# Gate projection spread over the inversion levels, and 64-row blocks for the GLA and RWKV states

## The reference

```python
u = rmsnorm(h, norm_mix);  proj = u @ w_in
y_rw  = rwkv7_mix(token_shift(proj[:, :1792]))     # 8 heads x 64
y_gla = gla_mix(proj[:, 1792:])                    # 4 heads, key 64, value 128
h = h + concat(y_rw, y_gla) @ w_out
h = h + moe(rmsnorm(h))                            # top 4 of 32 experts, 12.6 MB of weights each
h = h + sigmoid(rmsnorm(h) @ w_ple_gate) * (p @ w_ple);  out = rmsnorm(h)
# gla_mix, per chunk of 64 tokens:
o = (q * exp(b)) @ state + (tril(decayed q k^T)) @ v
state = exp(b_last) * state + (k * exp(b_last - b))^T @ v
o = o * rsqrt(mean(o*o)) * norm_g * silu(g)        # g: the 512 gate columns of proj
# rwkv7_mix, per token:
state = state * w + (state @ -kk) (kk*a)^T + v k^T;  o = state @ r
```

## Time and profile before

| | us |
|---|---|
| runs (3): median, lowest, highest | 1190.81, 1190.02, 1194.16 |
| the profiled execution | 1189.66 |
| its span from first to last instruction | 1187.9 |
| TensorE busy | 1121.3 |
| VectorE, ScalarE, GpSimd busy | 322.1, 217.9, 45.7 |
| HBM read in all | 430.57 MB |

### The profile page before, as it was taken

How to read it: one execution, slowest core, us unless ns; L and a number is a source line. 1 busy time by engine, 2 the same in 40 slices (tenths; PEclk the granted TensorE clock), 3 DMA queues, 4 the chain that set the end, 5 groups by cost and what they waited for, 6 DMA issues and landing times.

```text
span 1187.9 us, 15866 instructions
## 1 busy us (share of the span) xinstructions
PE 1121.3 (94%) x6255; PEld 504.7 (42%) x6255; DVE 322.1 (27%) x727; ACT 217.9 (18%) x394; POOL 45.7 (4%) x97
## 2 busy tenths in 40 slices
PE   8999899999999999998999889899999999999997
PEld 6876675433333433333333333333333333333344
DVE  2362366322222212122121221222222222222233
ACT  3233220221111111111111111111121111111124
POOL 8004200000000000000000000000000000000000
PEclk9999998999999999999999999999999999999999
DMA  9500328989999999999999999999999999999960
GB/s 326 196 1 1 135 100 336 359 353 429 429 428 429 428 429 428 429 428 430 426 430 427 429 428 429 428 429 427 430 428 429 428 428 429 427 429 428 428 282 37
DMA packets 41979, 432.11 MB, mean 364 GB/s; under 512 B 5300, under 2 KB 8696, under 8 KB 16824
## 3 DMA queue, kind: packets, MB, share of 16 engines
q1 hardware_dynamic: 41696, 431.34, 86.7%
q10 hardware_dynamic: 248, 0.29, 0.1%
HBM read 430.57 MB, written 1.05 MB: 363 GB/s over the span
## 4 chain that ended last, share of the span: by engine, by line
PE 57%; DMA 39%; DVE 1%; ACT 1%; issue 1%; POOL 1%; ACTq 0%; SPq 0%; DVEq 0%; POOLq 0%
PE ps L1209 53%; DMA ring<-in_w_dram 38%; PE ps L1752 1%; PE ps L1690 1%; DMA ay<-in_norm_ple_dram 0%; PE ps L1737 0%; PE ps L1624 0%; ACT ring L669 0%; ACTq L543 0%; PE ps L1454 0%; PE ps L1236 0%; PE ps L1608 0%; SPq L314 0%; PE ps L1333 0%; POOL ring L508 0%
## 5 line engine op out<-in xcount | busy, mean ns | idle before, releaser
L1209 PE MATMUL ps<-ring,ay 128*64 128x512 f32 x1024 | 245.4, 623 | 35.9 <-DMA ring<-in_w_dram 34.4
L1209 PE MATMUL ps<-ring,gqk 128*64 128x512 f32 x1024 | 224.3, 596 | 6.2 <-DMA ring<-in_w_dram 5.2
L1121 DVE COPY t<-ps 128x512 f32<-128x512 f32 x32 | 22.1, 691 | 505.7 <-PE ps L1209 505.7
L1209 PEld LDWEIGHTS ps<-ring,ay 128*64 128x64 f32 x1024 | 73.1, 142 | 183.7 <-issue 135.5
L1209 PEld LDWEIGHTS ps<-ring,gqk 128*64 128x64 f32 x1024 | 80.0, 138 | 147.5 <-issue 139.0
L1209 PE MATMUL ps<-ring,bu 128*128 128x512 f32 (+1 forms) x240 | 87.8, 520 | 1.1 <-DVE bu L793 1.0
L726 ACT ACTIVATE t<-ps 128x512 f32<-128x512 f32 x32 | 19.1, 597 | 361.0 <-PE ps L1209 361.0
L1209 PE MATMUL ps<-bu,ring 128*128 128x256 f32 (+2 forms) x328 | 68.9, 370 | 3.2 <-DVE ring L986 1.5
L1209 PEld LDWEIGHTS ps<-bu,ring 128*128 128x128 f32 (+1 forms) x328 | 60.1, 190 | 13.1 <-issue 1.8
L1209 PE MATMUL ps<-yb,ohgt 64*128 64x512 f32 x264 | 65.6, 615 | 0.0
L1209 PEld LDWEIGHTS ps<-ring,bu 128*128 128x128 f32 x240 | 45.5, 195 | 36.9 <-issue 32.7
(11 more groups left out here) (344 smaller groups left out, 826.2 us busy)
## 6 DMA issues: line engine op xcount, KB each, us to landing
ring<-in_w_dram SPq DMA_DIRECT2D x128, 2048.0 KB, 24.6
lg<-in_w_dram SPq DMA_DIRECT2D x16, 2048.0 KB, 25.7
bkv<-in_w_dram SPq DMA_DIRECT2D x16, 2048.0 KB, 30.7
ka<-in_w_dram SPq DMA_DIRECT2D x16, 2048.0 KB, 27.2
bu<-in_w_dram SPq DMA_DIRECT2D x16, 2048.0 KB, 28.6
ring<-in_w_in_dram SPq DMA_DIRECT2D x5, 2048.0 KB, 18.5
ring<-in_w_out_dram SPq DMA_DIRECT2D x1, 4096.0 KB, 13.8
ring<-in_w_ple_gate_dram SPq DMA_DIRECT2D x1, 4096.0 KB, 30.7
```

The lines of the kernel that those rows point to most:

```text
L1121: dve.tensor_copy(HS[:, 512:1024].rearrange("p (j q) -> p j q", j=4), bank(5).rearrange("p (q j) -> p j q", j=4)).then_inc(hs1, 1)
L1209: return pe.matmul(out_, lhs, rhs, start=start, stop=stop, skip_group_check=shared)
```

## The change

The gate projection keeps two of its products in each round of the `mats` loop; the other 16 (tile 1) are put between the steps of the five levels. SP's wait for its end goes from `gg_ps` 3 to 2 of two signals. The turns of X stand behind rounds 6 and 7 instead of each round; `MAT_BANKS` and the gate banks are swapped. GLA attention becomes 16 products of 64 x 64 in quadrants and goes into level 1. GLA's three added states are 12 products in level 2 and the carry is done at once on VectorE in level 3 (`gla_states`) with a per-partition scalar; `gla_intra` works by quadrants in level 4, and the reads of the state come in one piece (`gla_read`) after the levels, behind the two products of the RWKV gate. The sigmoid of the gate is made in two halves. `wu` is copied by VectorE and ScalarE, a bank each. RWKV's added terms and states are 64-row blocks (256 columns instead of 512), the identity product is replaced by an addition on VectorE (`carried`), and `out_intra` and `state` are interleaved in another order.

The diff, cut to its core:

```diff
 LEADS = ((0, 9, 4), (9, 12, 2), (12, NE // 2 - 1, 0))
 START = 1
-GO = (5, 7)
+GO = (4, 5)
 TOK_ORDER = (0, 1, 4, 5, 6, 7, 2, 3)
 MAT_ORDER = (2, 3, 4, 5, 6, 7, 0, 1)
-MAT_BANKS = ((4, 5), (2, 3))
-GG_ORDER = ((0, 1), (1, 1), (0, 0), (1, 0))
...
         QE, KE, QB, KL = (slot(8)[:, 512 * i:512 * (i + 1)].rearrange("p (h t) -> p h t", h=2) for i in range(4))
-        ATT = slot(9)[:, 0:1024].rearrange("p (t h w) -> p t h w", t=TT, h=GH)
-        KLT = slot(9)[:, 1024:1536].rearrange("p (t h w) -> p t h w", t=TT, h=2)
-        SG = slot(9)[:, 1536:2048]
+        ATT = slot(9)[:, 0:512].rearrange("p (j g w) -> p j g w", j=2, g=4)
...
         GTS = slot(11)[:, 1024:2048].rearrange("p (c h w) -> p c h w", c=2, h=HP)
-        HS_ = T34[:, 0:1536].rearrange("p (c w) -> p c w", c=3)
-        SRW = BK[:, 0:1536].rearrange("p (c h w) -> p c h w", c=3, h=HP)
+        HS_ = T34[:, 0:768].rearrange("p (c w) -> p c w", c=3)
+        SRW = BK[:, 0:768].rearrange("p (c h w) -> p c h w", c=3, h=HP)
+        GSQ = T34[:, 1024:2048]
...
-            sp.wait_ge(gg_ps, 3)
+            sp.wait_ge(gg_ps, 2)
...
-            sp.wait_ge(att_ok, 2)
-            sp.wait_ge(gate_ok, 2)
-            sp.wait_ge(wu_ok, 4)
+            sp.wait_ge(att_ok, 1)
+            sp.wait_ge(wu_v, 2)
+            sp.wait_ge(wu_a, 2)
...
-            sp.wait_ge(go_ps, 1)
+            sp.wait_ge(go_ps, 2)
             load_w2(0, 0)
-            sp.wait_ge(reff_ps, 2)
+            sp.wait_ge(reff_ps, 1)
             load_w1(0, 0, 1)
-            sp.wait_ge(o_ps, 1)
+            sp.wait_ge(o_ps, 3)
             sp.wait_ge(bv_ok, 1)
             sp.dma_start(B1R[0:NE, :], b1[0]).then_inc(b1_in, 16)
...
-            pool.wait_ge(gsig, 1)
+            pool.wait_ge(gsig, 2)
+            pool.wait_ge(gvg_ok, 4)
...
+            first_turned(1, 6)
+            gate_input(0)
+            first_turned(0, 8)
+            act.wait_ge(gla_ps, 1)
+            act.activation(KLT, bank(7).rearrange("p (t h w) -> p t h w", t=TT, h=2), ACT.Copy).then_inc(klt_ok, 1)
+            turned_x(0, 0)
+            turned_x(0, 1)
...
+            act.wait_ge(gvg_ok, 3)
+            act.activation(GSIG[:, 0:512], GG[:, 0:512], ACT.Sigmoid).then_inc(gsig, 1)
+            turned_x(1, 0)
+            turned_x(1, 1)
+            turned_x(2, 0)
+            turned_x(2, 1)
+            turned_x(3, 0)
+            turned_x(3, 1)
+            gate_input(1)
+            turned_x(4, 0)
+            turned_x(4, 1)
             for t in range(TT):
+                act.wait_ge(gate_ps, t + 1)
+                act.activation(GATE[:, 512 * t:512 * (t + 1)], bank(6 + t), ACT.Copy).then_inc(gate_ok, 1)
+            act.wait_ge(gvg_ok, 4)
+            act.activation(GSIG[:, 512:1024], GG[:, 512:1024], ACT.Sigmoid).then_inc(gsig, 1)
+            for t in range(TT):
+                act.wait_ge(wu_ps, t + 1)
+                act.activation(WU[:, :, t, 1:NH:2, :], bank(2 * t + 1).rearrange("p (u w d) -> p w u d", u=HP, w=2), ACT.Copy).then_inc(wu_a, 1)
+            act.wait_ge(go_ps, 2)
+            for j in range(2):
+                signal(act.activation(GSQ.rearrange("p (t q j w) -> p j t q w", t=TT, q=2, j=2)[:, j],
+                                      bank(GO[j]).rearrange("p (t q w) -> p t q w", t=TT, q=2), ACT.Square), osq_a)
...
+            def attention():
+                dve.wait_ge(gla_ps, 2)
+                signal(dve.tensor_tensor(ATT, bank(6, 2).rearrange("p (j r) -> p j r", j=2)[:, :, 0:256].rearrange("p j (g w) -> p j g w", g=4),
+                                         MK[:, 320:384].unsqueeze(1).unsqueeze(1).broadcast_to([P, 2, 4, L]), ALU.mult), att_ok)
+            def gla_states():
+                dve.wait_ge(gla_ps, 3)
+                link(dve.tensor_copy(SG[:, 0], bank(6)[:, 0:256].rearrange("p (q w) -> p q w", q=2)))
+                for c in (1, 2):
+                    for q in range(2):
+                        signal(dve.scalar_tensor_tensor(out=SG[:, c, q], in0=SG[:, c - 1, q], scalar=EM[:, 16 + 4 * q + c:17 + 4 * q + c],
+                                                        in1=bank(7 if c == 1 else 6)[:, 256 * (c // 2) + P * q:256 * (c // 2) + P * (q + 1)],
+                                                        op0=ALU.mult, op1=ALU.add))
+                    settle()
+                dve.memset(SM[:, 123:124], 0.0).then_inc(sg_ok, 1)
             for lv in range(5):
+                below(lv, 0)
+                below(lv, 1)
+                if lv == 2:
+                    attention()
+                if lv == 3:
+                    gla_states()
+                step(lv, 0)
+                step(lv, 1)
             for t in range(TT):
+                dve.wait_ge(wu_ps, t + 1)
+                dve.tensor_copy(WU[:, :, t, 0:NH:2, :], bank(2 * t).rearrange("p (u w d) -> p w u d", u=HP, w=2)).then_inc(wu_v, 1)
...
-                signal(dve.tensor_tensor(h4(HS_[:, c]), h4(bank(hb[c])), bdb, ALU.mult))
+                dve.wait_ge(h_ps, 2 if c == 2 else 1)
+                b = bank(7 if c == 1 else 6)[:, 256 * (c // 2):256 * (c // 2) + 256]
+                link(dve.tensor_copy(HS_[:, c], b), h_ok)
...
+            def carried(c):
+                link(dve.tensor_tensor(HS_[:, c], HS_[:, c], SRW[:, c - 1].rearrange("p h w -> p (h w)"), ALU.add))
...
+            added(2)
+            carried(2)
+            state(2)
...
+            def gg_part(first, last):
+                for i in range(first, last):
+                    t, half, k = i // 16, i // 8 % 2, i % 8
+                    ins = mm(bank(4 + t)[:, 256 * half:256 * (half + 1)], UT3[:, k, P * t:P * (t + 1)], cols(0 if half else 11, 256)[:, k, :],
+                             k == 0, k == KC - 1)
+                    if i % 16 == 15:
+                        ins.then_inc(gg_ps, 1)
...
+                gg_part(2 * n, 2 * n + 2)
+                if n == 6:
+                    for i in range(5):
+                        x_turned(i)
+                if n == 7:
+                    x_turned(5)
...
+            def attention():
+                pe.wait_ge(mv_ok, 2)
+                for t in range(TT):
+                    for q in range(2):
+                        for j in range(2):
+                            for c in range(2):
+                                tok = slice(P * t + L * c, P * t + L * (c + 1))
+                                ins = mm(bank(6 + j)[HALF[c], L * (2 * t + q):L * (2 * t + q + 1)], KE[HALF[j], q, tok], QE[HALF[j], q, tok])
...
+            def gla_added():
+                pe.wait_ge(att_ok, 1)
+                pe.wait_ge(klt_ok, 1)
+                pe.wait_ge(gvg_ok, 2)
+                for q in range(2):
+                    for c in (0, 1):
+                        for j in range(2):
+                            mm(bank(6 + c)[HALF[j], P * q:P * (q + 1)], KLT[HALF[c], 0, q, L * j:L * (j + 1)],
...
+            def gla_intra():
+                pe.wait_ge(gvg_ok, 4)
+                for swap in (1, 0):
+                    for t in range(TT):
+                        for q in range(2):
+                            for c in range(2):
+                                j = 1 - c if swap else c
+                                h = 2 * q + j
+                                ins = mm(bank(GO[j])[HALF[c], P * (2 * t + q):P * (2 * t + q + 1)], ATT[HALF[c], j, 2 * t + q, :],
+                                         GV[HALF[c], 512 * t + P * h:512 * t + P * (h + 1)], t == 0 and q == 0, False, True)
+                ins.then_inc(go_ps, 1)
+            def gla_read():
+                pe.wait_ge(sg_ok, 1)
+                pe.wait_ge(go_ps, 1)
+                for c in (1, 2, 3):
+                    t = c // 2
+                    for q in range(2):
+                        for j in range(2):
+                            ins = mm(bank(GO[j])[HALF[c % 2], P * (2 * t + q):P * (2 * t + q + 1)], QB[HALF[j], q, L * c:L * (c + 1)],
+                                     SG[HALF[j], c - 1, q, :], False, c == 3 and q == 1, True)
+                ins.then_inc(go_ps, 1)
...
+            x_turned(7)
+            levels_begin(0)
+            gla_keys()
+            gg_part(16, 17)
+            levels_step(0)
+            values()
+            levels_turn(0)
+            levels_begin(1)
+            gg_part(17, 20)
+            levels_step(1)
+            attention()
+            gg_part(20, 21)
+            levels_turn(1)
+            levels_begin(2)
+            gg_part(21, 24)
+            levels_step(2)
+            gla_added()
+            levels_turn(2)
+            levels_begin(3)
+            gg_part(24, 27)
+            levels_step(3)
+            gg_part(27, 30)
+            levels_turn(3)
+            levels_begin(4)
+            gg_part(30, 32)
+            levels_step(4)
+            gla_intra()
+            levels_turn(4)
+            gate_product(0)
+            gate_product(1)
+            gla_read()
...
             def added(cs):
-                for h in range(HP):
```

(52 more changed lines are left out.)

238 lines of the change are left out of this document (73 added, 165 removed).

## The result

The changed kernel takes 1180.24 us (median of four runs, 1178.46 to 1181.71); four runs of the kernel before have a median of 1191.22. The ratio is 0.9895, 95% interval 0.9878 to 0.9912: 11 us or 1.05% faster, where 15 us was forecast and 1170 to 1185 was the range. The profiled execution took 1180.11 us with a span of 1178.4, against 1189.66 and 1187.9.

What follows compares the result with a forecast made beforehand. The prediction took the end to be set by when TensorE reaches the b1 gate and the weight stream becomes full. 19.6 us earlier, less 2.0 and 2.6, gave 15.0 us: 1175.9 us for the median, likeliest 1176, range 1170 to 1185.

Steps and rivals of the forecast that it cites:

- The bound: A microsecond TensorE gains at the b1 gate is one at the end: 15.0 us at both.
- Loop and levels: From the mats loop through five levels: first level at 122.4 us, wu at 154.7, 11.0 us earlier.
- From wu to the output: Stretch from wu to the last output product: 14.1 us instead of 25.4, so output complete at 168.8 us.
- the unseen costs: Late instruction fetch, 2.0 us, and half clock, 2.6 us, subtracted from a gain of 19.6 us at the b1 gate.
- Fetch stops: TensorE through wu, added and transitions under full DMA: none or up to four stops of 2 us; one taken, 2.0 us.
- fetch stops pile up: Rival: three or four stops under full DMA from 148 to 169 us, 4 to 6 us more, 1180 to 1182; chance 0.16.
- Clock: Half clock after idle times at 166 and 169 us, ahead of the w_out products: none or 3.4 us lost; 2.6 taken.
- y_gla: TensorE waits for VectorE's y_gla, 5.55 us after REFF starts, at 171.4 us; 2.6 us of the gain given back.
- The other rivals: w_out late (4 us, 1180, chance 0.06); levels at 1.2 GHz (1203, 0.04); no added cost (1171.2, 0.15); no arrival (1189 to 1191, 0.03).
- The ceiling set by the transfers: Transfers queued up to the b1 gate drain at 189 us; a gain over 20 us would be cut off.

Runs made afterwards that it cites:

- gg_in_loop_late: Changed kernel with all 32 gate projection products back in the mats loop, and SP's loads held until below of level 4 is done: 1185.1 us.
- quiet: Changed kernel, but SP holds the first w1 chunk, x, w_out and all later loads until the last output product: 1189.8 us (one run).
- before_late: Kernel before, with SP's loads behind gg_ps held until below of level 4 is done: 1188.8 us, ratio 0.9966.
- wide_states: Changed kernel with the RWKV part undone (dense 128 x 128 blocks, identity product back): 1179.4 us, ratio 0.9888.
- early_rstd: Changed kernel with the GLA norm moved ahead of REFF on VectorE: 1178.5 us, ratio 0.9899.
- combo_late: Changed kernel with x loaded first, first w1 chunk behind w_out, GLA norm ahead of REFF, five unread products in the wait for REFF: 1177.5 us, ratio 0.9873.
- gg_in_loop: Changed kernel with all 32 gate projection products back in the mats loop, none in the levels: 1188.4 us, ratio 0.9968.
- late: Changed kernel with x loaded ahead of the gg_ps wait and the first w1 chunk issued behind w_out: 1177.6 us, ratio 0.9872.
- keep_busy: Changed kernel with 5 unread products in the wait for REFF and 10 behind the last output product: 1178.2 us, ratio 0.9884.
- x_first: Changed kernel with SP's load of x ahead of the wait for gg_ps 2: 1179.4 us, ratio 0.989.
- wide_best: Changed kernel with dense RWKV blocks, x first, GLA norm ahead of REFF, six unread products, b1 loaded behind the first w2 chunk: 1173.7 us, ratio 0.9858.

## Why the prediction was right, and where it was off

**The bound.** Right in kind. A shift of TensorE at the b1 gate is a shift of the end, but not all of it arrives: 11.9 us at the gate, 10.2 at the first gather's transposes (236.70 to 226.48), 9.6 in the two profiled executions and 11 in the medians. The prediction called itself wrong if gate and end differed by over 2 us; in the profiled pair they differ by 2.3. Of these 1.7 us are a second stretch at half clock between the gate and the router, which I hadn't in the sum; the other 0.6, in the stream of the experts, has no cause shown.

**Loop and levels.** Right, within 0.3 us of the clock: first level at 122.4 as forecast, `wu` at 154.4 where 154.7 was forecast. Some of that is luck: this profile's loop started 0.45 us earlier than that of the kernel before, and counted from the first `mats` the gain up to `wu` is 10.8 us where 11.0 was forecast. Two terms in it were wrong and cancelled: `gla_intra` took 1.86 us, not 0.96, which is 116 ns a product, as for two at a time, and not 60 as for four; the two G2 products and `gla_read` together took 2.3 us, not 3.1. The reason for the worth of the spread holds: I had the first microsecond of filler in a level as nearly free. With 16 gate products (7.3 us by the forecast's price) the five levels take 29.8 us, in gg_in_loop_late without them 28.7, of which some 2 are the stop and the half clock told above. So 4 to 6 of the 7.3 us cost nothing, about the microsecond a level.

**From wu to the output: the term that was mis-sized.** Forecast 14.1 us without the unseen costs. Quiet shows 15.7 us with neither stops nor half clock. Of the missing 1.6 us 1.1 is `state`: four products of 64 columns with 128 x 128 weights took 1.03 us each time, not 0.5. Halving the columns from 128 to 64 brought nothing there. The rest, some 0.5, is net of small differences: `wu` with the tail of `gla_read` 2.3 us instead of 1.9, and a wait of 0.2 for VectorE.

```profile
161.95 1.10 PE L1238 MATMUL ps<-bu,ring 128*128 128x64 f32 x8
```

**Fetch stops: right in kind, half in size.** One of 2.0 us was taken; three of 3.96 us came, just under the 4 us that the prediction had named as a sign of being wrong, and what the rival "fetch stops pile up" had. I argued against it with the 480 instructions that passed from 169 to 180 us before. That comparison is the step that failed, for two reasons. First, w_out's transfer only began at 169.5 there: one instruction packet had passed at 167.4, ahead of it, and the next, at 176.0, was for a block that TensorE, by the count of records in before_late, needed only at 178.6, just before its wait for REFF. before_late has the same products with the burst already running, and it stopped for 0.17 and 0.93 us. Second, the change made the products quick: the packets pass 6.6, 6.1 and 6.5 us apart there, and 127 records took 5.56 and 4.03 us. wide_states, with 7.3 us for 128, had no stop.

**Clock: right in place, short in size.** 2.6 us were taken. Measured against the same products at full clock the first stretch cost 0.84 us in `out_state` (2.11 against quiet's 1.27), 0.94 in the transposes and 0.85 in the products, 2.6 in all. That this equals the forecast is in part luck, for the forecast had it follow the two waits, and it began with the stop ahead of them. The waits can do it too: early_rstd has the stop without the wait for `y_gla`, wide_states the two waits without a stop, and both had half clock. The second stretch, 1.7 us, was not foreseen.

**y_gla.** REFF to `y_gla` took 5.55 us, as forecast, and `y_gla` released the transposes, as named. The times of the two are late by the stops: the last output product ended at 175.4 where 169 to 171 was forecast, the b1 transposes at 196.4 where 192 to 194 was.

Added up: 1.1 for `state`, some 0.5 for `wu` and small waits, 2.0 for more stops, 1.7 for the second stretch, less 0.3 in the levels is 5.0 us; the sum had 15.0 and the profiled pair shows 9.6, so 0.4 us is left over, less than what profiles of one kernel differ by. The other rivals are out: w_out never released TensorE, and the levels ran at full clock. The ceiling set by the transfers was there as described: combo_late ran into it.

## What to carry to other kernels

Before shortening small products that run beside full transfers, count instructions as well as columns: here 34 products fewer and twice the columns were worth the same, and the fastest kernel was built on them, though the 64-row blocks were never run with the same other edits. A check that can be made ahead of time is how long TensorE takes for 128 of its records: where that was less than the distance of the instruction packets it stopped. A wait in the DMA queue's program is a tool of the same rank as the order of products: holding 4 MB back from a dense stretch of small products brought `wu` 3.5 us forward with one line, and a small transfer that is needed early belongs ahead of the large ones. When a chain is shortened, look at what the neighbours on the other engines do in the freed time (VectorE's norm waited behind REFF while VectorE had been idle for 6 us) and at which queued transfer becomes the next to be waited for.

## What the runs showed of the hardware

- TensorE stops of up to 4.0 us without a releaser come when it passes small products quickly. All 27 told of above end 2.3 to 2.7 us after an instruction packet, and consecutive ones stand 127 or 128 records apart. With the DMA share at about 1 the packets passed 6.1 to 6.6 us apart in the changed kernel and 6.0 and 6.2 in wide_states; the stops vanish when either the transfers (quiet) or the rate of instructions (wide_states) goes down. The longest, 3.98 us, came in the levels of gg_in_loop. With no data moving there was one, of 0.46 us (gg_in_loop_late), where the packets were 3.8 us apart.
- The clock was at 1.2 GHz in, or within 2 us of the end of, each stop of 1.5 us or more. It fell without a stop behind waits of 1.81 and 2.18 us in wide_states, and behind one of 1.78 us in gg_in_loop_late. In the changed kernel the first stretch cost 2.6 us, in wide_states 1.7. It also fell behind the b1 gate in some profiles (the changed kernel twice, early_rstd, late, keep_busy, combo_late, gg_in_loop_late, before_late), for 1.4 to 2.9 us, and not in others with nearly the same order (before, quiet, x_first, wide_states, wide_best, gg_in_loop). The pause just before those products is 1.0 us in all but wide_states, which had 1.35 and kept its clock; combo_late had a wait of 1.67 ahead of its b1 transposes besides. What decides it stays open.
- Four products with 128 x 128 weights take 1.03 us with 64 columns each and 0.99 with 128 (176.34 to 177.33 us in the kernel before); fewer columns saved nothing in `state`.
